# The first loads, splits and bias products in another order, and a feed-forward statistic one job later

## The chip, the cores and the metric

The kernel runs on one core of one Trainium2 chip. The metric is the device time of one execution in microseconds (us). Engines are named as in the profile: PE is TensorE, DVE is VectorE, ACT is ScalarE, POOL is GpSimd, SP is SyncE, which here only issues transfers.

## The reference, cut to what matters

The kernel computes two stacks of transformer blocks over 512 tokens with 1024 features, in float32. The part that matters here is the feed-forward network (FFN) that opens and closes each of the two layers of the first block, and once more closes the second block:

```
def rmsnorm(x, g, eps=EPS):
    y = x * rsqrt(mean(x * x, axis=-1) + eps)
    return y * g

x = x + 0.5 * (silu(rmsnorm(x, g) @ w_gate) * (rmsnorm(x, g) @ w_up)) @ w_down      # layers 0 and 1, twice each
...
rel_bias: (32 buckets, 10 heads), read by bucket of the relative position, for the attention logits
```

D_FF is 2816, that is 22 tiles of 128 columns for the gate and 22 for the up projection. Between the two FFNs of a layer lie mixers (a Fourier branch, dilated window attention, a dense differential attention). The tables of position biases are made once, at the start, from rel_bias and a 0/1 table.

## The kernel before

**Products.** Every large matrix product is done on the feature-major activations: a "job" multiplies one 1024x128 block of weights (eight tiles of 128x128) with the 512 tokens into one PSUM bank. For precision, weights and activations are each split into a high part (a rounded copy, type fp32r) and a low part (what is left), and each tile takes three matmuls: high x high, low x high, high x low (lines 646 to 648). A job is thus 24 matmuls of 512 columns.

**Weights.** Two slots, s = 0 and 1, hold the weights of two jobs. For each half of a slot, SP loads `raw` from the list `jobs` (line 482), ACT copies it to `w_hi` (`split`, line 1398), POOL subtracts to get `w_lo` (`low`, line 513), and PE may then use the half. ACT may overwrite `w_hi` only when PE has finished that half of the job before in the slot (semaphores `job_half`, `job_done`). `pump(s)` on ACT is both halves of one slot. PE waits for `lo_done` ahead of each half of a job, in order of its program.

**Banks.** A job in slot s writes bank s. DVE takes the result out (`scaled`, line 2127) and multiplies it by `rs`, the reciprocal root mean square of each token; the norm is applied after the product, so jobs can begin before `rs` exists. PE waits for that (`evac`) before it writes the bank again.

**The norm's statistic.** While an FFN's input tiles are made, ACT squares each (line 1412) and DVE sums the squares in `acc` (line 2115). `statistic` on PE (line 702) sums `acc` over the partitions with a matmul by ones, directly behind job 0 of the FFN. ACT then takes the square root (`deviation`, line 1417) and DVE the reciprocal (line 2122). In the last FFN of all (`ffn("tiles")`) the statistic is made of small matmuls inside job 0.

**The FFN on each engine.** PE: job 0, statistic, job 1, then a loop of job 0 and job 1 for each further tile, in parts of 6, 8 and 8 tiles with a down projection behind each. ACT's program for the first tile of an FFN is `before()`, `deviation()`, `pump(0)`, the silu of the gate (line 1425), and then for each further tile `pump(1)`, `upper` (m_hi, line 1430), `pump(0)`, silu. Each engine works strictly in the order of its program. DVE: reciprocal, then per tile the two `scaled`, the product (line 2144) and `lower` (m_lo, line 2137).

**The start.** SP loads the small constants, the four parts of x (512 KB each), then the weights of the first two jobs in four halves. ACT issues the transfers of the 0/1 table `hot` (33 rows of 1920), of `rel_bias`, of the lambda vectors and of an identity. PE waits for those, does one small product for lambda (line 1371) and four products of 33 rows with 512 or 384 columns (line 1374), which give the bias vectors, and then begins the first layer. ACT and DVE prepare the eight x tiles in turn: square, high part, sum, low part; ACT waits for each sum before the next square, as there is one buffer for squares. `pump(0)` stands behind the second tile, `pump(1)` behind the eighth.

Of the kernel before, what the change touches and what calls it, by code (L numbers as in the profile page):

```python
# [109 lines left out]
VEC = {0: (0, 1024), 1: (1024, 384), 2: (1408, 256), 3: (1664, 256)}  # L110
VEC_COLS = 1920
HEAD_OF = [6, 7, 8, 9, 0, 1, 2, 3, 4, 5]
KIND_OF = [0, 0, 0, 0, 1, 1, 2, 2, 3, 3]
# [32 lines left out]
def constants():  # L146

    c = {}
    k, n = np.arange(P), np.arange(S)
    a = 2 * np.pi * (k[:, None] * k[None, :] % P) / P  # L150
    j = np.arange(EVEN)
    even = 2 * np.pi * (k[:, None] * 2 * j[None, :] % S) / S
    odd = 2 * np.pi * (k[:, None] * (2 * j[None, :P] + 1) % S) / S
    even_sin, odd_sin = np.sin(even), np.sin(odd)
    even_sin[:, [0, P]] = 0
    odd_sin[0] = 1 - 2 * (j[:P] % 2)
    middle = np.zeros((P, 8, EVEN))
    for g in range(8):
        middle[g, g] = 1 - 2 * (j % 2)
    c["dft"] = np.concatenate([np.cos(a) / 256, np.sin(a) / 256, np.cos(even), np.cos(odd), even_sin, odd_sin,  # L160
                               middle.reshape(P, -1)], 1)
    hot = np.zeros((33, VEC_COLS))
    for kind, (at, size) in VEC.items():
        i = np.arange(size)
        rel, ok = ((i - 511, i < 1023), (i - 191, abs(i - 191) <= 64), (4 * (i - 127), abs(i - 127) <= 64),
                   (4 * (i - 127), (i - 127) % 4 == 0))[kind]
        hot[bucket(rel), at + i] = ok
        hot[32, at + i] = np.where(ok, 0, -1e30)
    for at, size in VEC.values():
        hot[:, at:at + size] = hot[:, at:at + size][:, ::-1].copy()  # L170
    c["hot"] = hot
# [44 lines left out]
def build(nc, jobs, x_in, small_in, mem_in, pos_in, rel_in, lam_in, dft_in, hot_in, eye_in,  # L216
          window_in, chunk_in, swap_in, rows8_in, out):
    NJ = jobs.shape[0]
    with ExitStack() as ctx:
# [3 lines left out]
        def sem(name):  # L223
# [45 lines left out]
            key_squared key_sums bc_full bc_read columns_ready fill_full fill_copied mem_loaded  # L269
            input_squared input_added mem_squared mem_added query_norms"""  # L270
        (loaded, setup_in, mixer_in, tile_squared, par_ready, vec_ready, vec_stored, tab_full, silu_done, h_done,
# [7 lines left out]
         columns_ready, fill_full, fill_copied, mem_loaded, input_squared, input_added, mem_squared, mem_added,  # L279
         query_norms) = [sem(n) for n in names.split()]  # L280
        lane_names = """rows_in cross_full chunk_terms decay_done next_ready level_full turn_copied level_done
# [29 lines left out]
        rows_z = flat[0:2, VB * S:(VB + 3) * S].rearrange("p (g n) -> p g n", g=3)  # L311
        hot = flat[0:33, 0:VEC_COLS]
        relb = pt[0:33, 4, 0:10]
        lamv = pt[0:64, 5, 0:8]
# [157 lines left out]
        def _(sp):  # L472
            sp.dma_start(small[:, :], small_in).then_inc(loaded, 16)
            for i in range(4):
                sp.dma_start(x[:, 2 * i:2 * i + 2], x_in[:, 2 * i:2 * i + 2]).then_inc(x_in_part[i], 16)

            def refill(i):
# [5 lines left out]

            refill(0)
            refill(1)
# [24 lines left out]
        def _(pool):  # L510
# [85 lines left out]

            jobs_low(0, LANE_JOBS // 2)
            for s in range(4):
# [27 lines left out]
        def _(pe):  # L626
# [757 lines left out]
        def _(act):  # L1384
# [675 lines left out]
            act.dma_start(hot, hot_in).then_inc(setup_in, 16)  # L2060
            act.dma_start(pt[0:32, 4, 0:10], rel_in).then_inc(setup_in, 16)
            act.dma_start(lamv, lam_in).then_inc(setup_in, 16)
            act.dma_start(eye[:, :], eye_in).then_inc(mixer_in, 16)
            act.wait_ge(loaded, 16)
            for k in range(KT):
                if k:
                    act.wait_ge(acc_step, k)
                if k == 2:
                    pump(0)
                prepare(k, small[:, TAIL["g_first"] + k:TAIL["g_first"] + k + 1], (x_in_part[k // 2], 16))  # L2070
                if k == 0:
                    act.wait_ge(vec_ready, 1)
                    act.activation(stats[:, 0:4], ps[6][:, 0:4], ACT.Exp).then_inc(lam_done, 1)
            pump(1)
            act.wait_ge(vec_ready, 2)
            for i in range(2):
                copy = act.activation(vec_sb[:, i * 512:i * 512 + 512], ps[2 + i][0:10, :], ACT.Copy)
            copy.then_inc(vec_copied, 1)
# [10 lines left out]
        def _(dve):  # L2089
# [11 lines left out]
            dve.memset(eps[:, 1:2], 1e-5).then_inc(par_ready, 1)  # L2101
            dve.memset(relb[32:33], 1.0).then_inc(par_ready, 1)
            dve.wait_ge(dve_step, c.now("dve"))
# [19 lines left out]

            def scaled(s, dst):

                dve.wait_ge(job_done[s], c.next(f"job{s}"))
                dve.tensor_tensor(dst, ps[s][:, :], rs[:, :], ALU.mult).then_inc(evac[s], c.up(f"evac{s}"))  # L2127

# [9 lines left out]

            def ff_tile(k):
                scaled(0, gr)  # L2140
                scaled(1, ur)
# [18 lines left out]
            def ffn(gain):  # L2160
                reciprocal_rms()
                for part, n in enumerate(FF_PARTS):
                    with c.loop(dve, n, {**JOB, "silu": 1, "h": 1, "m_hi": 1, "m": 1}) as i:
                        ff_tile(i)
                    if part < 2:
# [300 lines left out]
            def second():  # L2466
# [41 lines left out]
                for part, n in enumerate(FF_PARTS):  # L2508
                    with c.loop(dve, n, {**JOB, "silu": 1, "h": 1, "m_hi": 1, "m": 1}) as i:
                        ff_tile(i)  # L2510
                    if part == 0:
# [419 lines left out]
            for k in range(KT):  # L2931
                dve.wait_ge(x_in_part[k // 2], 16)
                prepare(k, small[:, TAIL["g_first"] + k:TAIL["g_first"] + k + 1])
            dve.wait_ge(vec_ready, 2)
            for i in range(2, 4):
                n = min(512, VEC_COLS - i * 512)
                copy = dve.tensor_copy(vec_sb[:, i * 512:i * 512 + n], ps[2 + i][0:10, 0:n])
            copy.then_inc(vec_copied, 1)
# [14 lines left out]

def arrays_of(i):
# [37 lines left out]
    for n, v in tail.items():  # L2995
# [13 lines left out]
        "pos_in": i["positions_2"],  # L3009
        "rel_in": i["rel_bias"],  # L3010
        "lam_in": np.stack([i[n][l] for l in range(2) for n in ("lam_q1", "lam_q2", "lam_k1", "lam_k2")], 1),
# [16 lines left out]
```

## Time and profile before

| | |
|---|---|
| median of 3 runs | 3389.3 us (3389.01 to 3389.61) |
| span of the profiled execution | 3389.0 us, 0.3 us below that median |
| PE busy | 3340.8 us, 99% of the span |
| POOL, DVE, ACT busy | 1568.5, 1449.3, 1351.6 us |
| HBM read | 309.64 MB |

The profiled execution's own time is taken as its span; nothing around it is known beyond the 0.3 us. Busy time of PE counts overlapping matmuls once. All times of rows are from the start of the span.

### The profile page before, as it was taken

How to read it: one execution, taken by the hardware profiler on the slowest of the kernel's cores; microseconds unless marked ns; L12 is line 12 of the kernel's file. 1: busy time of each engine (PE TensorE's matmuls, PEld its weight loads, DVE VectorE, ACT ScalarE, POOL GpSimd, SP SyncE). 2: the span in 40 equal slices, each digit the busy share in tenths (PEclk: the TensorE clock that was granted, in tenths of full speed). 3: DMA queues.
4: the chain of work that ended last, by engine and by line, in shares of the span. 5: the costliest groups of instructions: out<-in, count | busy, mean ns of one | idle time of the engine just before them, and what ended most of it. 6: DMA issues, size and time to landing. Idle time of an engine off the chain costs nothing.

```text
span 3389.0 us, 52959 instructions
## 1 busy us (share of the span) xinstructions
PE 3340.8 (99%) x16934; PEld 2729.1 (81%) x16934; DVE 1449.3 (43%) x2241; ACT 1351.6 (40%) x2414; POOL 1568.5 (46%) x1198
## 2 busy tenths in 40 slices
PE   8999999999999999999999999999999999999999
PEld 6888888788888888888888788888877787778887
DVE  4223622655322342324434644232478676342323
ACT  4323324654432343334235634332447554333332
POOL 4544443345454445444433354544433356255444
PEclk9999999999999999999999999999999999999999
DMA  3332322233232233223222233323322123123322
GB/s 124 108 97 96 118 88 69 73 103 99 96 109 96 96 97 109 96 96 119 96 75 76 68 115 97 110 94 100 98 76 71 46 73 107 50 73 109 97 96 87
DMA packets 175224, 313.65 MB, mean 93 GB/s; under 512 B 19121, under 2 KB 28337, under 8 KB 175096
## 3 DMA queue, kind: packets, MB, share of 16 engines
q1 hardware_dynamic: 163172, 298.09, 27.3%
q10 hardware_dynamic: 11924, 13.86, 1.6%
q8 instruction: 80, 1.31, 0.2%
q14 instruction: 48, 0.39, 0.0%
HBM read 309.64 MB, written 2.23 MB: 92 GB/s over the span
## 4 chain that ended last, share of the span: by engine, by line
PE 94%; DVE 2%; issue 2%; ACT 1%; POOL 1%; ACTq 0%; DMA 0%; SPq 0%; DVEq 0%; POOLq 0%
PE ps L646 25%; PE ps L648 25%; PE ps L647 25%; PE ps L685 2%; PE ps L687 2%; PE ps L686 2%; PE ps L856 1%; PE ps L667 1%; PE ps L669 1%; PE ps L668 1%; PE ps L871 1%; PE ps L1049 1%; PE ps L736 0%; PE ps L863 0%; PE ps L653 0%
## 5 line engine op out<-in xcount | busy, mean ns | idle before, releaser
L513 POOL TENSOR_TENSOR w_lo<-raw,w_hi 128x512 fp32r<-128x512 f32 x1120 | 1488.0, 1334 | 1734.3 <-ACT w_hi L1398 1729.2
L1398 ACT ACTIVATE w_hi<-raw 128x512 fp32r<-128x512 f32 x1120 | 693.4, 628 | 1293.2 <-PE ps L648 1192.7
L646 PE MATMUL ps<-u_hi,w_hi 128*128 128x512 f32 (+1 forms) x2902 | 1140.7, 393 | 7.4 <-DVE u_lo L2410 4.1
L648 PE MATMUL ps<-u_lo,w_hi 128*128 128x512 f32 (+1 forms) x2902 | 1124.8, 388 | 0.0
L647 PE MATMUL ps<-u_hi,w_lo 128*128 128x512 f32 (+1 forms) x2902 | 1124.6, 388 | 0.0
L646 PEld LDWEIGHTS ps<-u_hi,w_hi 128*128 128x128 f32 x2902 | 546.4, 188 | 129.4 <-issue 15.7
L647 PEld LDWEIGHTS ps<-u_hi,w_lo 128*128 128x128 f32 x2902 | 546.4, 188 | 113.4 <-issue 5.4
L648 PEld LDWEIGHTS ps<-u_lo,w_hi 128*128 128x128 f32 x2902 | 546.1, 188 | 112.5
L2127 DVE TENSOR_TENSOR T<-ps,rs 128x512 f32<-128x512 f32 x268 | 185.1, 691 | 733.2 <-PE ps L648 730.5
L646 PE MATMUL ps<-m_hi,w_hi 128*128 128x512 f32 x964 | 378.3, 392 | 2.4 <-DVE m_lo L2487 1.3
L647 PE MATMUL ps<-m_hi,w_lo 128*128 128x512 f32 x964 | 375.2, 389 | 0.0
L648 PE MATMUL ps<-m_lo,w_hi 128*128 128x512 f32 x964 | 375.1, 389 | 0.0
L646 PEld LDWEIGHTS ps<-m_hi,w_hi 128*128 128x128 f32 x964 | 181.0, 188 | 46.8 <-DVE m_lo L2487 5.3
L2149 DVE SCALAR_TENSOR_TENSOR x<-ps,x 128x512 f32 x112 | 77.4, 691 | 322.0 <-PE ps L648 265.2
L648 PEld LDWEIGHTS ps<-m_lo,w_hi 128*128 128x128 f32 x964 | 181.0, 188 | 37.9
L647 PEld LDWEIGHTS ps<-m_hi,w_lo 128*128 128x128 f32 x964 | 181.0, 188 | 37.5 <-issue 0.7
L2144 DVE TENSOR_TENSOR T<-T 128x512 f32<-128x512 f32 x110 | 188.0, 1709 | 20.7 <-DVE T L2127 17.4
L1430 ACT ACTIVATE m_hi<-T 128x512 f32 (+1 forms) x130 | 82.3, 633 | 277.3 <-DVE T L2144 217.3
L2137 DVE TENSOR_TENSOR m_lo<-T,m_hi 128x512 f32 (+1 forms) x130 | 92.7, 713 | 113.9 <-ACT m_hi L1430 113.9
L2127 DVE TENSOR_TENSOR pt<-ps,rs 128x512 f32<-128x512 f32 (+1 forms) x83 | 57.1, 688 | 183.0 <-PE ps L648 182.4
L687 PE MATMUL ps<-m_lo,w_hi 128*128 128x512 f32 x252 | 98.0, 389 | 0.0
L685 PE MATMUL ps<-m_hi,w_hi 128*128 128x512 f32 x252 | 98.0, 389 | 0.0
(492 smaller groups left out, 3033.8 us busy)
## 6 DMA issues: line engine op xcount, KB each, us to landing
raw<-jobs SPq DMA_DIRECT2D x1120, 256.0 KB, 2.7
tab<-vec_dram ACTq DMA_DIRECT2D x8, 448.0 KB, 5.7
pt<-rows_dram ACTq DMA_DIRECT2D x9, 256.0 KB, 4.8
x<-x_in SPq DMA_DIRECT2D x4, 512.0 KB, 6.9
out<-x SPq DMA_DIRECT2D x8, 256.0 KB, 2.3
tab<-dft_in ACTq DMA_DIRECT2D x2, 901.0 KB, 4.7
pt<-share_dram ACTq DMA_DIRECT2D x4, 384.0 KB, 4.7
T<-rows_dram ACTq DMA_DIRECT2D x3, 256.0 KB, 5.3
```

The lines of the kernel that those rows point to most:

```text
L513: pool.tensor_tensor(w_lo[:, s, w], raw[:, s, w], w_hi[:, s, w].bitcast(F32), ALU.subtract).then_inc(lo_done[s], 1)
L646: pe.matmul(ps[bank][:, 0:n], w_hi[:, s, w], hi[:, k, 0:n], start=k == ks[0], stop=False)
L647: pe.matmul(ps[bank][:, 0:n], w_lo[:, s, w], hi[:, k, 0:n], start=False, stop=False)
L648: last = pe.matmul(ps[bank][:, 0:n], w_hi[:, s, w], lo[:, k, 0:n], start=False, stop=k == ks[-1])
L685: pe.matmul(ps[s][:, :], w_hi[:, s, w], hi[:, k], start=k == 0, stop=False)
L687: last = pe.matmul(ps[s][:, :], w_hi[:, s, w], lo[:, k], start=False, stop=k == n - 1)
L1398: act.activation(w_hi[:, s, half_of(half)], raw[:, s, half_of(half)], ACT.Copy).then_inc(hi_done[s], 1)
L1430: act.activation(tile(m_hi, k), hf if src is None else src, ACT.Copy).then_inc(m_hi_done, c.up("m_hi"))
L2127: dve.tensor_tensor(dst, ps[s][:, :], rs[:, :], ALU.mult).then_inc(evac[s], c.up(f"evac{s}"))
L2137: dve.tensor_tensor(tile(m_lo, k), hf if src is None else src, tile(m_hi, k).bitcast(F32), ALU.subtract).then_inc(m_ready, c.up("m"))
L2144: dve.tensor_tensor(hf, sg, ur, ALU.mult).then_inc(h_done, c.up("h"))
L2149: dve.scalar_tensor_tensor(out=tile(x, k), in0=ps[s][:, :], scalar=scale, in1=tile(x, k), op0=ALU.mult, op1=ALU.add).then_inc(evac[s], c.u ...
```

## The change

It does three things. At the start, SP interleaves the weight halves of the first job with the parts of x, and ACT makes the high parts of all tiles, and the splits of the first job, ahead of the squares; POOL squares tiles 0 to 2 and ACT tiles 3 to 7, each into a buffer of its own. The four bias products become row tiles: the 0/1 table is cut into four strips of 480 columns that lie on 32 partitions each, so each product uses its own 32 rows of PE's array (the row for unreached positions takes the place of bucket 15, which no position has). In every FFN, the third and fourth job write banks 2 and 3 without a wait for the first pair's results, and in the FFNs of the two layers the statistic is behind job 1 instead of behind job 0. The diff, cut to its core:

```diff
@@ constants: 32 rows, four strips of 480 columns
-    hot = np.zeros((33, VEC_COLS))
+    hot = np.zeros((32, VEC_COLS))
...
+    c["hot"] = np.concatenate(np.split(hot, 4, 1))
@@ SP
-            for i in range(4):
-                sp.dma_start(x[:, 2 * i:2 * i + 2], x_in[:, 2 * i:2 * i + 2]).then_inc(x_in_part[i], 16)
+            first_weights(0, 0)
+            first_inputs(0)
+            first_inputs(1)
+            first_weights(0, 1)
+            first_inputs(2)
+            first_inputs(3)
+            first_weights(1, 0)
+            first_weights(1, 1)
-            refill(0)
@@ POOL
-            jobs_low(0, LANE_JOBS // 2)
+            first_low(0, 0)
+            first_input_square(0)
+            first_input_square(1)
+            first_low(0, 1)
+            first_input_square(2)
+            first_low(1, 0)
+            first_low(1, 1)
+            jobs_low(1, LANE_JOBS // 2)
@@ PE, ffn
-                        job(0, u_hi, u_lo, ready=ready, stat=stat)
+                        job(0, u_hi, u_lo, ready=ready, stat=stat == "tiles" and stat)
                         job(1, u_hi, u_lo)
-                    with c.loop(pe, n - (part == 0), PJOB):
+                        if stat is True:
+                            statistic()
+                        pe.wait_ge(vec_copied, 2)
+                        for s in range(2):
+                            c.take(f"evac{s}")
+                            product(s, 2 + s, u_hi, u_lo, range(KT)).then_inc(job_done[s], c.up(f"job{s}"))
+                    with c.loop(pe, n - 2 * (part == 0), PJOB):
@@ PE, start
-            pe.wait_ge(par_ready, 3)
+            pe.wait_ge(par_ready, 2)
...
-                n = min(512, VEC_COLS - i * 512)
-                mm = pe.matmul(ps[2 + i][0:10, 0:n], relb, hot[:, i * 512:i * 512 + n], start=True, stop=True)
+                rows = slice(32 * i, 32 * i + 32)
+                mm = pe.matmul(ps[2 + i][0:10, 0:VEC_STRIP], relb[rows], hot[rows], start=True, stop=True, tile_position=(32 * i, 0))
@@ ACT, start
-            for k in range(KT):
-                if k:
-                    act.wait_ge(acc_step, k)
-                if k == 2:
-                    pump(0)
-                prepare(k, ...)
+            split(0, 0)
+            for k in range(2):
+                first_upper(k)
+            act.wait_ge(vec_ready, 1)
+            act.activation(stats[:, 0:4], ps[6][:, 0:4], ACT.Exp).then_inc(lam_done, 1)
+            for k in range(2, 4):
+                first_upper(k)
+            split(0, 1)
+            for k in range(4, KT):
+                first_upper(k)
             pump(1)
+            for k in range(len(POOL_SQUARES), KT):
+                act.activation(first_square[:, k], x[:, k], ACT.Square).then_inc(square_done, c.up("square"))
@@ DVE, ffn (both places)
+                    apart = 2 if part == 0 else 0
+                    for i in range(apart):
+                        ff_tile(i, 2 * i)
+                    with c.loop(dve, n - apart, ...) as i:
+                        ff_tile(i + apart)
@@ DVE, start: all eight low parts first, then the eight sums
```

`rel_bias` is given four times over (128 rows of 10), one copy for each strip. ACT's program for the FFNs (`before()`, `deviation()`, `pump(0)`, silu) is not touched.

## Rows read from the trace of the kernel before

**Rows 1.** The page: busy time by engine, and the chain that ended last.
```profile
PE 3340.8 (99%) x16934; PEld 2729.1 (81%) x16934; DVE 1449.3 (43%) x2241; ACT 1351.6 (40%) x2414; POOL 1568.5 (46%) x1198
...
PE 94%; DVE 2%; issue 2%; ACT 1%; POOL 1%; ACTq 0%; DMA 0%; SPq 0%; DVEq 0%; POOLq 0%
```

**Rows 2.** Timeline of layer 1's first FFN: start, length, engine, line, [idle before].
```profile
1240.21 1.02 PE L702 MATMUL ps<-T,ones 128*128 128x512 f32 x2
...
1241.27 0.69 ACT L1417 ACTIVATE T<-ps,eps 128x512 f32<-128x512 f32 x1 [0.71 <-PE ps L702]
1241.30 0.40 PE L647 MATMUL ps<-u_hi,w_lo 128*128 128x512 f32 x1
...
1241.85 1.14 ACT L1398 ACTIVATE w_hi<-raw 128x512 fp32r<-128x512 f32 x2
...
1242.55 2.54 POOL L513 TENSOR_TENSOR w_lo<-raw,w_hi 128x512 fp32r<-128x512 f32 x2 [2.35 <-ACT w_hi L1398]
...
1246.62 0.49 PE L646 MATMUL ps<-u_hi,w_hi 128*128 128x512 f32 x1
...
1247.70 2.99 POOL L513 TENSOR_TENSOR w_lo<-raw,w_hi 128x512 fp32r<-128x512 f32 x2 [2.61 <-ACT w_hi L1398]
```

**Rows 3.** Timeline, PE: the second FFNs of layer 0 and of layer 1.
```profile
879.77 1.02 PE L702 MATMUL ps<-T,ones 128*128 128x512 f32 x2
...
885.66 0.39 PE L647 MATMUL ps<-u_hi,w_lo 128*128 128x512 f32 x1
885.89 0.39 PE L648 MATMUL ps<-u_lo,w_hi 128*128 128x512 f32 x1
886.15 0.49 PE L646 MATMUL ps<-u_hi,w_hi 128*128 128x512 f32 x1
...
2094.60 1.02 PE L702 MATMUL ps<-T,ones 128*128 128x512 f32 x2
...
2100.98 0.49 PE L646 MATMUL ps<-u_hi,w_hi 128*128 128x512 f32 x1
```

**Rows 4.** Timeline of the start and the first FFN.
```profile
9.50 0.56 PE L1371 MATMUL ps<-pt,ones 64*128 64x4 f32 x2 [9.50 <-DVE pt L2927]
9.98 6.57 PE L1374 MATMUL ps<-pt 33*10 33x512 f32 x8
16.48 0.80 PE L646 MATMUL ps<-u_hi,w_hi 128*128 128x512 f32 x1
...
20.06 0.60 PE L648 MATMUL ps<-u_lo,w_hi 128*128 128x512 f32 x1
20.49 0.41 PE L646 MATMUL ps<-u_hi,w_hi 128*128 128x512 f32 x1
...
22.85 1.14 DVE L2937 COPY pt<-ps 10x512 f32<-10x512 f32 x2
...
23.94 1.02 PE L702 MATMUL ps<-T,ones 128*128 128x512 f32 x2
...
31.23 0.49 PE L646 MATMUL ps<-u_hi,w_hi 128*128 128x512 f32 x1 [0.79 <-DVE T L2127]
```

**Rows 5.** Timeline, PE: two groups of eight matmul passes.
```profile
634.89 1.99 PE L856 MATMUL ps<-pt 64*128 64x512 f32 x8
...
2948.99 3.70 PE L1363 MATMUL ps<-T,pt 128*128 128x512 f32 x8 [0.69 <-ACT T L2057]
```

**Rows 6.** Stretches of two pauses of PE: PE, PEld, DVE, ACT, POOL busy, PEclk, DMA, GB/s.
```profile
2952.70:2954.10 1.40, 0.00 (x0) 0.00 (x0) 0.74 (x2) 1.09 (x2) 0.00 (x0) 1.00 0.00 0
2954.20:2957.00 2.80, 2.80 (x12) 2.08 (x12) 1.63 (x3) 0.34 (x1) 0.00 (x0) 1.00 0.00 0
...
2957.00:2959.30 2.30, 0.15 (x2) 0.01 (x1) 1.29 (x2) 1.89 (x5) 1.41 (x2) 1.00 0.00 0
2959.40:2962.80 3.40, 3.40 (x9) 2.63 (x9) 1.62 (x1) 1.01 (x2) 3.40 (x3) 0.50 0.45 152
```

**Rows 7.** Stretch of the start, same columns: transfers while x is loaded.
```profile
5.00:10.00 5.00, 0.50 (x3) 0.52 (x4) 0.81 (x4) 2.52 (x3) 0.00 (x0) 1.00 1.02 378
```

More of the change, by code:

```diff
@@ L111 @@
 VEC_COLS = 1920
+VEC_STRIP = VEC_COLS // 4
+UNREACHED = 15
 HEAD_OF = [6, 7, 8, 9, 0, 1, 2, 3, 4, 5]
@@ L167, in constants @@
         hot[bucket(rel), at + i] = ok
-        hot[32, at + i] = np.where(ok, 0, -1e30)
+        hot[UNREACHED, at + i] = np.where(ok, 0, -1e30)
     for at, size in VEC.values():
         hot[:, at:at + size] = hot[:, at:at + size][:, ::-1].copy()
-    c["hot"] = hot
+    c["hot"] = np.concatenate(np.split(hot, 4, 1))
     c["eye"] = np.eye(P)
@@ L279, in build @@
          columns_ready, fill_full, fill_copied, mem_loaded, input_squared, input_added, mem_squared, mem_added,
-         query_norms) = [sem(n) for n in names.split()]
+         query_norms, first_squares) = [sem(n) for n in names.split()]
         lane_names = """rows_in cross_full chunk_terms decay_done next_ready level_full turn_copied level_done
@@ L311, in build @@
         rows_z = flat[0:2, VB * S:(VB + 3) * S].rearrange("p (g n) -> p g n", g=3)
-        hot = flat[0:33, 0:VEC_COLS]
-        relb = pt[0:33, 4, 0:10]
+        hot = pt[:, 0, 0:VEC_STRIP]
+        relb = pt[:, 4, 0:10]
+        first_square = pt[:, 8:16]
+        POOL_SQUARES = (0, 1, 2)
         lamv = pt[0:64, 5, 0:8]
@@ L473, in _, with first_weights, first_inputs @@
             sp.dma_start(small[:, :], small_in).then_inc(loaded, 16)
-            for i in range(4):
+            def first_weights(s, half):
+                w = half_of(half)
+                sp.dma_start(raw[:, s, w], jobs[s, :, w]).then_inc(raw_full[s][half], 16)
+            def first_inputs(i):
                 sp.dma_start(x[:, 2 * i:2 * i + 2], x_in[:, 2 * i:2 * i + 2]).then_inc(x_in_part[i], 16)
+            first_weights(0, 0)
[6 more added lines that the diff above has]
+            first_weights(1, 1)
             def refill(i):
@@ L595, in lane_low, with first_low, first_input_square @@
                         memory_sum(k)
-            jobs_low(0, LANE_JOBS // 2)
+            def first_low(s, half):
+                pool.wait_ge(hi_done[s], half + 1)
+                low(s, half)
+            def first_input_square(k):
+                pool.wait_ge(x_in_part[k // 2], 16)
+                pool.tensor_tensor(first_square[:, k], x[:, k], x[:, k], ALU.mult).then_inc(first_squares, 1)
+            first_low(0, 0)
[6 more added lines that the diff above has]
+            jobs_low(1, LANE_JOBS // 2)
             for s in range(4):
@@ L2064, in _, with first_upper @@
             act.wait_ge(loaded, 16)
-            for k in range(KT):
-                if k:
-                    act.wait_ge(acc_step, k)
-                if k == 2:
-                    pump(0)
[L2070 to L2073, printed above, removed]
+            def first_upper(k):
+                act.wait_ge(x_in_part[k // 2], 16)
+                gain = small[:, TAIL["g_first"] + k:TAIL["g_first"] + k + 1]
+                act.activation(u_hi[:, k], x[:, k], ACT.Copy, scale=gain).then_inc(u_hi_done, c.up("u_hi"))
+            split(0, 0)
[8 more added lines that the diff above has]
+                first_upper(k)
             pump(1)
+            for k in range(len(POOL_SQUARES), KT):
+                act.activation(first_square[:, k], x[:, k], ACT.Square).then_inc(square_done, c.up("square"))
             act.wait_ge(vec_ready, 2)
             for i in range(2):
-                copy = act.activation(vec_sb[:, i * 512:i * 512 + 512], ps[2 + i][0:10, :], ACT.Copy)
+                copy = act.activation(vec_sb[:, i * VEC_STRIP:(i + 1) * VEC_STRIP], ps[2 + i][0:10, 0:VEC_STRIP], ACT.Copy)
             copy.then_inc(vec_copied, 1)
@@ L2122, in reciprocal_rms, with scaled @@
                 step(dve.reciprocal(rs[:, 0:n], std[:, 0:n]))
-            def scaled(s, dst):
+            def scaled(s, dst, bank=None):
                 dve.wait_ge(job_done[s], c.next(f"job{s}"))
-                dve.tensor_tensor(dst, ps[s][:, :], rs[:, :], ALU.mult).then_inc(evac[s], c.up(f"evac{s}"))
+                dve.tensor_tensor(dst, ps[s if bank is None else bank][:, :], rs[:, :], ALU.mult).then_inc(evac[s], c.up(f"evac{s}"))
             def scaled_keys(s, dst):
@@ L2137, in lower, with ff_tile @@
                 dve.tensor_tensor(tile(m_lo, k), hf if src is None else src, tile(m_hi, k).bitcast(F32), ALU.subtract).then_inc(m_ready, c.up("m"))
-            def ff_tile(k):
-                scaled(0, gr)
-                scaled(1, ur)
+            def ff_tile(k, bank=0):
+                scaled(0, gr, bank)
+                scaled(1, ur, bank + 1)
                 dve.wait_ge(evac[1], c.now("evac1"))
@@ L2162, in ffn @@
                 for part, n in enumerate(FF_PARTS):
-                    with c.loop(dve, n, {**JOB, "silu": 1, "h": 1, "m_hi": 1, "m": 1}) as i:
-                        ff_tile(i)
+                    apart = 2 if part == 0 else 0
+                    for i in range(apart):
+                        ff_tile(i, 2 * i)
+                    with c.loop(dve, n - apart, {**JOB, "silu": 1, "h": 1, "m_hi": 1, "m": 1}) as i:
+                        ff_tile(i + apart)
                     if part < 2:
@@ L2508, in second @@
                 for part, n in enumerate(FF_PARTS):
-                    with c.loop(dve, n, {**JOB, "silu": 1, "h": 1, "m_hi": 1, "m": 1}) as i:
-                        ff_tile(i)
+                    apart = 2 if part == 0 else 0
+                    for i in range(apart):
+                        ff_tile(i, 2 * i)
+                    with c.loop(dve, n - apart, {**JOB, "silu": 1, "h": 1, "m_hi": 1, "m": 1}) as i:
+                        ff_tile(i + apart)
                     if part == 0:
@@ L2932, in _ @@
                 dve.wait_ge(x_in_part[k // 2], 16)
-                prepare(k, small[:, TAIL["g_first"] + k:TAIL["g_first"] + k + 1])
+                dve.wait_ge(u_hi_done, c.next("u_hi"))
+                dve.scalar_tensor_tensor(out=u_lo[:, k], in0=x[:, k], scalar=small[:, TAIL["g_first"] + k:TAIL["g_first"] + k + 1],
+                                         in1=u_hi[:, k].bitcast(F32), op0=ALU.mult, op1=ALU.subtract).then_inc(u_ready, c.up("u"))
+            for k in range(KT):
+                if k in POOL_SQUARES:
+                    dve.wait_ge(first_squares, k + 1)
+                else:
+                    dve.wait_ge(square_done, c.next("square"))
+                if k:
+                    dve.wait_ge(acc_step, c.now("acc"))
+                dve.tensor_tensor(acc, acc, first_square[:, k], ALU.add).then_inc(acc_step, c.up("acc"))
             dve.wait_ge(vec_ready, 2)
             for i in range(2, 4):
-                n = min(512, VEC_COLS - i * 512)
-                copy = dve.tensor_copy(vec_sb[:, i * 512:i * 512 + n], ps[2 + i][0:10, 0:n])
+                copy = dve.tensor_copy(vec_sb[:, i * VEC_STRIP:(i + 1) * VEC_STRIP], ps[2 + i][0:10, 0:VEC_STRIP])
             copy.then_inc(vec_copied, 1)
@@ L2952, in _, with bias_table @@
             second()
+def bias_table(rel):
+    one = np.ones((1, rel.shape[1]), np.float32)
+    return np.concatenate([rel[:UNREACHED], one, rel[UNREACHED + 1:]] * 4)
 def arrays_of(i):
@@ L3009, in arrays_of @@
         "pos_in": i["positions_2"],
-        "rel_in": i["rel_bias"],
+        "rel_in": bias_table(i["rel_bias"]),
         "lam_in": np.stack([i[n][l] for l in range(2) for n in ("lam_q1", "lam_q2", "lam_k1", "lam_k2")], 1),
```

5 lines of the change are left out of this document (2 added, 3 removed).

## The prediction

> **What bounds the kernel now.** I read the page first: PE is busy for 99% of the span, and the chain that ended last is 94% PE [rows 1]. So time can only come from places where PE pauses or runs at a lower clock, and any new pause is paid in full, because nothing later waits for anything slower than PE. Then I read PE's waits over the whole span: near the change they are the 9.5 us before the first product and 0.79 us before the third job of the first FFN [rows 4]. The starts of the other FFNs I read as timelines [rows 2, 3]. In layer 0's second FFN the matmul after job 1 starts 0.26 us behind the last one, against 0.23 in a steady row: a pause of 0.03 us. So the wait for the first pair's results, which the extra banks remove, costs almost nothing there. The reader should look at what ACT does behind the statistic instead: it waits for PE's statistic, takes the root, and only then makes w_hi for the third job [rows 2].
>
> **The change, part by part.**
>
> *The statistic behind job 1.* ACT's program is unchanged: deviation, then pump(0). pump(0) makes the weights of the third job, so in the new order that job's weights can't be split before the statistic, and the statistic now comes directly ahead of the job. The chain is read from before, counted from the start of the statistic [rows 2]: root begins 1241.27 - 1240.21 = 1.06 us later; first split 0.58 after that (1241.85); first low part 0.70 after that (1242.55); it takes 2.54 / 2 = 1.27. So lo_done comes at 1.06 + 0.58 + 0.70 + 1.27 = 3.61, and with a semaphore's latency, for which I put 0.07, PE goes on 3.68 us after the statistic began. The root starts right behind the statistic, so the table load for it, which ACT does while it waits, stays hidden.
>
> What this costs: before, from the start of the statistic to the third job, which holds the statistic and job 1, took 886.15 - 879.77 = 6.38 us [rows 3] in layer 0's second FFN and the same, 2100.98 - 2094.60, in layer 1's second, and 1246.62 - 1240.21 = 6.41 in layer 1's first [rows 2]. Job 1 alone is 24 matmuls at the spacing of 0.227 (885.66 to 885.89 rounds to 0.23) [rows 3], 5.45. After the change it is 5.45 + 3.68 = 9.13. The loss is 2.75 + 2.75 + 2.72 = 8.2 us over these three FFNs. In the first FFN before took 31.23 - 23.94 = 7.29 [rows 4], as DVE was late there, so the loss is 9.13 - 7.29 = 1.8. Together 10.0 us. Of the 9.13 us PE stands still for about 3.68 - 0.86 = 2.8 us; 0.86 is the statistic itself: the second matmul of job 1 starts at 1241.30, less one spacing for the first, less 1240.21 [rows 2].
>
> Queued behind ACT's wait are the split of slot 0, silu, and the split of slot 1. Is the fourth job late too? Its weights need silu, which needs the reciprocal. Before, the second pair of low parts began 1247.70 - 1240.21 = 7.49 us after the statistic [rows 2], at 2.99 / 2 = 1.5 each, so the first half is there at 9.0. The third job ends at 3.68 + 5.45 = 9.13. They meet; I put 0, and 0.4 each as the upper end.
>
> *Banks 2 and 3.* They remove the pauses of 0.03 to 0.06 and the 0.8 of the first FFN, already in the differences above. The wait for vec_copied falls on copies that start at 22.85 [rows 4] and will hardly be later, while the third job comes near 30. The FFN with "tiles" keeps its statistic within job 0 and gains nothing. The loop's next job waits for the evacuation of bank 2, which DVE does while the fourth job runs: the same cover as in any steady pair.
>
> *The clock.* After a pause of 2.3 us with hardly any matmul, the granted clock was 0.50 for the 3.4 us from 2959.4, that is 1.2 instead of 2.4 GHz; after the pause of 1.4 us before 2954.1 it stayed at 1.00 [rows 6]. There are four new pauses of 2.8 us, longer than the one that led to the fall. In those 3.4 us eight matmuls ran at 0.43 instead of 0.23, a cost of 1.6. Not every pause need be followed by it and part of the low stretch may fall into the pause; I take 1.1 each, 4.4 in all, between 0 and 6.4.
>
> *The start.* Before, the bias products run from 9.98 to 16.48, eight passes, 0.85 each for 512 columns [rows 4]; everything the first job needs is there earlier but for the products themselves. Now a pass has 480 columns: 0.80. One behind another they would take 6.4; all four tiles beside each other two steps, 1.6. Row groups can overlap here: eight passes on alternating halves of 64 rows took 1.99, eight on all rows 3.70 [rows 5]. But matmuls are issued in order, and both passes of a tile use the same rows, so tile i+1 can begin only beside tile i's second pass: five steps, 4.0 us. I take this value; 1.99 over 3.70 in place of one half says that order costs something. They begin when hot, rel_bias and lambda have landed. These now compete with 256 KB of weights put ahead of x (0.7 us at 378 GB/s [rows 7]) and are 128 rows each in place of 33 and 32; I put 1.2 us later, between 0 and 2. So the first job starts at 9.98 + 1.2 + 4.0 = 15.2 in place of 16.48: a lead of 1.3, between 4.9 (9.98 + 1.6) and -1.9 (9.98 + 2 + 6.4). The first job still starts at 1.2 GHz: before it ran 4.0 us at 0.43 spacing, from 16.48 to 20.49 [rows 4]; I put the same.
> Here a rule can be weighed. The Trainium skill, "TensorE: Matmul & The Clock Gate", section "Part 3: Packing small matmuls", gives a measured 3.07 times for four row tiles of 32 rows. By that the products would take 6.4 / 3.07 = 2.1 us, an estimate, and the lead would be 3.2; the trace has no four-tile case, only the two halves.
>
> The moved work doesn't bind. POOL does a low part in 1.3 to 1.5 us, and a square should take the same; with low, two squares, low, square, low, low, the second half of job 0 is split well ahead of PE, which needs 12 matmuls of 0.43 for the first half, and slot 1 is ready about 3 us before job 1. DVE's eight low parts and eight sums are 16 operations of some 0.7 us, done near 21, while the statistic, now behind job 1, is due near 28. If that cover were gone, each late microsecond would be one of PE.
>
> **Sum.** 3389.0 + 10.0 (waits) + 4.4 (clock) - 1.3 (lead) = 3402.1 for the profiled execution; with its 0.3 below the median, 3402.4.
>
> **The rivals.**
> 1. *The four tiles run beside each other.* Two steps of 0.80: products end at 9.98 + 1.2 + 1.6 = 12.8, lead 3.7, time 3400.0. For it: the halves overlap at all. Against: two passes per tile in order. The skill's figure above belongs to it.
> 2. *The pauses come but the clock holds.* 3389.3 + 10.0 - 1.3 = 3398.0. For it: 1.4 us didn't lower it, and 2.8 is not much above 2.3. With the full lead of 4.9 it would be 3394.4, within 0.2%.
> 3. *The fourth job is late too*, as DVE and POOL get in each other's way (low parts 2.99 for two in place of 2.54). 4 x 0.4 to 1 us: 3404 to 3406.
> 4. *The other side: the weights of the third job don't wait for the statistic*, because ACT reaches pump(0) first. Then nothing is lost, the pause of 0.8 and those of 0.03 go, and so does 1.3 at the start: 3389.3 - 0.9 - 1.3 = 3387.1, and 3383.5 with the full lead. It decides if w_hi of the third job lies before the root in ACT's order. Against: before, w_hi was free to be made from the end of job 0 and still began 0.58 behind the root [rows 2].
>
> **How the numbers follow.** Chances: forecast 0.56, rival 1 0.14, rival 2 0.14 (of which 0.04 with so large a lead that it is within 0.2%), rival 3 0.10, rival 4 0.06 (half of it faster by over 0.2%, since its start could gain more than I see). 0.2% is 6.8 us, about what a measurement of this kernel can tell from no change. Slower: 0.56 + 0.14 + 0.10 + 0.10 = 0.90; same 0.07; faster 0.03. The range: from 3396, which leaves out rival 4 and the low end of rival 2, to 3407, the sum with the clock at its full 6.4 and the lead at 0 plus 1 for rival 3.
>
> **What would show it.** In the changed profile, the four statistics (line of `statistic`) are each followed by a PE idle near 2.8 us, released by POOL's w_lo; root, w_hi and w_lo follow in steps of 1.06, 0.58, 0.70. The granted clock reads 0.50 for some microseconds behind most of them. The first job starts near 15.2 us, the bias passes take near 4 us. The first u_hi matmul of job 2 in the FFN with "tiles" shows no idle. The prediction is wrong if w_hi for slot 0 starts before the root, or if the first job starts before 12 us.

## The result and the profile after

| | before | changed |
|---|---|---|
| median | 3389.45 us (4 runs) | 3403.55 us (3399.87 to 3405.85, 4 runs) |
| ratio, 95% interval | | 1.0040 (1.0028 to 1.0052) |
| span of the profiled execution | 3389.0 us | 3400.1 us (that execution took 3401.9) |

The kernel became slower by 0.4%, and the forecast of 3402.4 lies 1.2 us from the median. Over the later comparisons the kernel before spreads more than its first runs showed: 3385.8 to 3394.1 in 33 runs, median 3390.2. So differences of 1 or 2 us are read from timelines below and not from times.

The time of an execution was 1.8 to 2.3 us above its span in every run where both are on record (3401.9 against 3400.1 here). So spans are compared with spans: 3400.1 - 3389.0 = 11.1 us is what the two profiles can explain. The two medians lie 14.1 us apart, which leaves 3 us that no timeline here shows; the interval of the ratio, 9.5 to 17.6 us, holds both.

PE's two longest waits in the changed kernel (line, whom it waited for, us in total, times, longest):

```profile
PE ps L678 <- POOL w_lo L530: 13.6, 6, 2.6
PE ps L1409 <- DVE pt L2978: 10.1, 1, 10.1
```

The wait for POOL's w_lo, the low parts of the weights, was 3.0 us in two pieces before and is now 13.6 in six. Four of them, of 2.6 us each, stand behind the statistics. The timeline of layer 1's first FFN answers to [rows 2]:

```profile
1248.61 1.02 PE L734 MATMUL ps<-T,ones 128*128 128x512 f32 x2
1249.67 0.69 ACT L1455 ACTIVATE T<-ps,eps 128x512 f32<-128x512 f32 x1 [6.76 <-PE ps L734]
1250.26 1.14 ACT L1436 ACTIVATE w_hi<-raw 128x512 fp32r<-128x512 f32 x2
...
1250.95 2.50 POOL L530 TENSOR_TENSOR w_lo<-raw,w_hi 128x512 fp32r<-128x512 f32 x2 [7.59 <-ACT w_hi L1436]
...
1252.27 0.50 PE L678 MATMUL ps<-u_hi,w_hi 128*128 128x512 f32 x1 [2.64 <-POOL w_lo L530]
```

The steps are 1.06, 0.59, 0.69 and 1.32 us, 3.66 in all, and PE idles 2.64 of them. (In a merged row of two, such as the last of POOL, each takes about half: PE goes on when the first low part is there.) ACT has been idle for 6.76 us when the statistic comes: it had time for the split, but its program puts the root first.

The same timeline at the start answers to [rows 4]:

```profile
10.06 0.56 PE L1409 MATMUL ps<-pt,ones 64*128 64x4 f32 x2 [10.06 <-DVE pt L2978]
...
10.54 1.79 PE L1412 MATMUL ps<-pt 32*10 32x480 f32 x8
...
12.26 0.80 PE L678 MATMUL ps<-u_hi,w_hi 128*128 128x512 f32 x1
...
14.40 5.58 DVE L2985 SCALAR_TENSOR_TENSOR u_lo<-x,small,u_hi 128x512 fp32r<-128x512 f32 x4
...
17.68 0.50 PE L678 MATMUL ps<-u_hi,w_hi 128*128 128x512 f32 x1 [0.73 <-DVE u_lo L2985]
19.38 0.50 PE L678 MATMUL ps<-u_hi,w_hi 128*128 128x512 f32 x1 [0.73 <-DVE u_lo L2985]
...
19.91 6.25 DVE L2994 TENSOR_TENSOR T<-T,pt 128x512 f32<-128x512 f32 x8
...
26.30 1.04 PE L734 MATMUL ps<-T,ones 128*128 128x512 f32 x2
...
29.98 0.50 PE L678 MATMUL ps<-u_hi,w_hi 128*128 128x512 f32 x1 [2.64 <-POOL w_lo L530]
```

The four bias products take 1.8 us in place of 6.6, the first job starts at 12.26 in place of 16.48, and the first statistic stands at 26.30, where in the old start job 1 would have ended at 23.94 + 5.45 = 29.39 (an estimate; experiment 6 has it at 29.41). Job 0 is now held up by the low parts of x (`u_lo`, DVE): three of its tiles start late, at 15.98, 17.68 and 19.38, by 2.0 us together. The third job starts at 29.98, 1.25 us ahead of before.

Pauses and the granted clock (columns as in [rows 6]):

```profile
27.30:29.90 2.60, 0.04 (x1) 0.00 (x0) 1.99 (x7) 2.50 (x4) 1.24 (x2) 1.00 0.22 30
30.70:34.10 3.40, 3.40 (x10) 2.65 (x9) 3.14 (x4) 1.09 (x3) 0.47 (x1) 0.50 0.49 156
886.60:889.20 2.60, 0.06 (x1) 0.00 (x0) 1.78 (x1) 2.48 (x4) 1.22 (x1) 1.00 0.00 0
889.40:892.80 3.40, 3.40 (x15) 2.81 (x16) 3.15 (x4) 1.50 (x4) 1.09 (x1) 1.00 0.43 151
1249.60:1252.20 2.60, 0.03 (x1) 0.00 (x0) 1.81 (x1) 2.51 (x4) 1.25 (x2) 1.00 0.01 3
1252.70:1256.10 3.40, 3.40 (x10) 2.66 (x9) 3.02 (x4) 1.50 (x3) 1.02 (x2) 0.50 0.47 154
```

Three pauses of equal length: behind the first and the third the granted clock was 0.50 (1.2 GHz) in the 3.4 us shown and 10 matmuls fell into them, behind the second it stayed at 1.00 (2.4 GHz) with 15. The fourth, in layer 1's second FFN, was like the second (1.00, 16 matmuls in 2111.1 to 2114.5).

The difference of the two spans can be added up from the statistics. Their starts in the two timelines, in us; where the statistic moved behind job 1, the column "less job 1" takes one job (5.45) off again, so that like is compared with like:

| statistic of | before | changed | changed, less job 1 | stage before it grew by |
|---|---|---|---|---|
| layer 0 mixers | 385.68 | 386.15 | | 0.47 (from 0) |
| layer 0 second FFN | 879.77 | 885.64 | 880.19 | -0.05 |
| layer 1 first FFN | 1240.21 | 1248.61 | 1243.16 | 2.53 |
| layer 1 mixers | 1600.51 | 1607.79 | | 4.33 |
| layer 1 second FFN | 2094.60 | 2107.27 | 2101.82 | -0.06 |
| second block | 2454.75 | 2464.70 | | 2.73 |

The last column says how much longer the stage ahead of that statistic became. 9.95 us are gathered by there. The remaining 1.1 of the 11.1 arise behind the second block's statistic. That last stretch took 934.3 us before and 935.4 changed, but 932.2 to 937.6 over the twelve profiled executions of this study, with no order by edit: the kernels of experiments 5 and 6 lead at that statistic by 2.2 and 1.0 us and end 0.6 and 2.4 behind. The granted clock is low in several stretches of this part, in every one of the twelve, and they lie elsewhere each time. So the 1.1 can't be put down to the change, and much of the spread of the times may come from there.

### The profile page after: what moved, and what is told of

Read it like the earlier page. It is cut to its first block, busy times and chain, and to the rows that moved or that the text cites. A ratio compares the mean times of both kernels' runs of the same rounds, so it can differ in the third digit from the quotient of the medians.

```text
span 3400.1 us, 52494 instructions
## 1 busy us (share of the span) xinstructions
PE 3340.4 (98%) x16934; PEld 2730.5 (80%) x16934; DVE 1453.1 (43%) x2240; ACT 1349.2 (40%) x2411; POOL 1571.7 (46%) x1201
## 4 chain that ended last, share of the span: by engine, by line
PE 92%; issue 3%; DVE 2%; POOL 1%; ACT 1%; ACTq 0%; DMA 0%; DVEq 0%; POOLq 0%
PE ps L678 25%; PE ps L680 25%; PE ps L679 25%; PE ps L717 2%; PE ps L719 2%; PE ps L718 2%; PE ps L894 1%; PE ps L699 1%; PE ps L701 1%; PE ps L700 1%; PE ps L909 1%; POOL w_lo L530 1%; PE ps L1087 1%; PE ps L774 0%; PE ps L901 0%
## 5 line engine op out<-in xcount | busy, mean ns | idle before, releaser
L678 PE MATMUL ps<-m_hi,w_hi 128*128 128x512 f32 x964 | 378.6, 393 | 2.4 <-DVE m_lo L2535 1.3
L679 PE MATMUL ps<-m_hi,w_lo 128*128 128x512 f32 x964 | 375.4, 389 | 0.0
L718 PE MATMUL ps<-m_hi,w_lo 128*128 128x512 f32 x252 | 98.1, 389 | 0.0
```

What stands on the lines that cost most here:

```text
L678: pe.matmul(ps[bank][:, 0:n], w_hi[:, s, w], hi[:, k, 0:n], start=k == ks[0], stop=False)
L679: pe.matmul(ps[bank][:, 0:n], w_lo[:, s, w], hi[:, k, 0:n], start=False, stop=False)
L718: pe.matmul(ps[s][:, :], w_lo[:, s, w], hi[:, k], start=False, stop=False)
```

## The experiments

Each is compared with runs of the kernel before, taken beside it on the same chip. The line numbers are those of each kernel. The edits are cut to what matters.

**1. The statistic behind job 0 again** (rest of the change kept).

```diff
-    job(0, ..., ready=ready, stat=stat == "tiles" and stat)
+    job(0, ..., ready=ready, stat=stat)
     job(1, u_hi, u_lo)
-    if stat is True:
-        statistic()
```

> The changed kernel with one thing undone: the FFN's statistic is again behind job 0. Theory (the pause behind the statistic is the loss, ACT's root ahead of the third job's split): the four pauses of 2.6 us and the falls of the clock behind them go in the three later FFNs, -8.2 us and most of the clock's 3 to 6. In the first FFN a new wait comes: the eight sums end at 26.16 in the changed profile, while job 0 ends near 20.7, so PE waits some 5.5 us there and the third job starts near 26.3 + 0.86 + 5.45 = 32.6 instead of 29.98, with a fall of the clock likely. Time 3390 to 3393. Rival (the loss lies in banks 2 and 3 or in the start): it stays at 3399 to 3405.

Measured: 3392.82 us, ratio 1.0009 (1.0000 to 1.0018). The theory holds in both parts. The waits of 2.6 us are gone in the three later FFNs. The wait that it foresaw in the first FFN is there, and the clock was low behind it (the statistic took 2.07 in place of 1.04), so the third job starts at 33.66 and not near 32.6:

```profile
19.52 6.25 DVE L2992 TENSOR_TENSOR T<-T,pt 128x512 f32<-128x512 f32 x8
25.83 2.07 PE L734 MATMUL ps<-T,ones 128*128 128x512 f32 x2 [5.18 <-DVE T L2992]
```

So the new start makes the sums late, and this is what a statistic behind job 1 covers in the one FFN that needs it; the other three pay for it.

**2. The split of slot 0 ahead of the root.**

```diff
     before()
-    deviation()
-pump(0)
+    pump(0)
+    deviation()
 gate(gr, sg, 0, ACT.Silu)
...
```

> The changed kernel, but in ACT's FFN program the split of slot 0 comes ahead of the root. Theory A (the third job's weights are the only thing late): the pauses of 2.6 go, as do the falls of the clock: 3403.5 - 4 x 2.8 - 3 to 5 = 3387 to 3390. Theory B (the pause only moves to the fourth job, whose split still stands behind the silu, which needs the reciprocal): in the changed profile the second pair of low parts starts 7.2 us after the statistic (1255.82 - 1248.61) and the first half is ready at 8.6; the third job would end at 0.86 + 5.45 = 6.3, so PE pauses 2.3 us one job later, clock falls included: 3403.5 - 4 x 0.4 = 3402. I hold B likelier.

Measured: 3400.57, ratio 1.0035 (1.0021 to 1.0048). Theory B. In layer 1's first FFN the third job follows the statistic at once, and the pause stands one job later:

```profile
1252.03 1.02 PE L734 MATMUL ps<-T,ones 128*128 128x512 f32 x2
1252.49 0.80 PE L678 MATMUL ps<-u_hi,w_hi 128*128 128x512 f32 x1
...
1259.25 2.99 POOL L530 TENSOR_TENSOR w_lo<-raw,w_hi 128x512 fp32r<-128x512 f32 x2 [9.54 <-ACT w_hi L1436]
...
1260.59 0.50 PE L678 MATMUL ps<-u_hi,w_hi 128*128 128x512 f32 x1 [2.05 <-POOL w_lo L530]
```

In the first FFN PE also waited 1.72 us for the sums, ahead of a statistic at 28.56: this edit already brings the wait that experiment 5 shows.

**3. The FFN part of the change alone**, on the old start (the PE and DVE hunks for the FFN).

> The kernel before with only the FFN part of the change: statistic behind job 1, third and fourth job in banks 2 and 3; the start as it was. Theory: 10.0 us of waits as in the prediction (2.75, 2.75, 2.72 and 1.8 in the first FFN) plus the clock's 0 to 6.4: 3389.4 + 10.0 + 3 = 3402.5, between 3399 and 3406. The first FFN's third job starts near 23.94 + 5.45 + 3.68 = 33.1. Rival (the start holds part of the loss): below 3399.

Measured: 3406.00, ratio 1.0049 (1.0036 to 1.0063), at the upper end. The statistic came at 30.23 and not at 29.4; of that, 0.6 us is the wait ahead of the first product, 10.1 here and 9.5 in [rows 4]. The FFN part alone makes the whole loss. The new start gives some of it back in the timelines (the third job is at 33.89 here and at 29.98 in the changed kernel); in the times, 3406.00 and 3403.55, the intervals overlap.

**4. The pauses filled.**

```diff
     pe.wait_ge(vec_copied, 2)
+    if stat is True:
+        for _ in range(11):
+            pe.matmul(ps[6][:, :], u_hi[:, 0, 0:P], u_hi[:, 0], start=True, stop=True)
```

> The changed kernel with eleven more matmuls of 512 columns on PE between statistic and third job, into a bank that nobody reads; 11 x 0.227 = 2.5 us lies inside the pause of 2.6 to 2.8. Theory (low clock behind the pauses costs 1.6 us each time it falls, and pauses cause it): the clock stays at 1.00 behind all four, the time is 3389.4 + 8.2 (three later FFNs) - 1.3 (third job of the first FFN) = 3396.3, and up to 1 more where a filler delays the third job; the spread of the changed kernel's runs (6 us) shrinks to that of before (about 1 us). Rival (the clock adds nothing, the rest is something else): 3401 to 3404 as before.

Measured: 3397.39, ratio 1.0020 (1.0011 to 1.0030), against 1.0040 (1.0028 to 1.0052) for the change. The third job still waits for the same chain, 3.69 us behind the statistic, but the clock holds:

```profile
1247.31 1.02 PE L734 MATMUL ps<-T,ones 128*128 128x512 f32 x2
1247.76 3.10 PE L760 MATMUL ps<-u_hi 128*128 128x512 f32 x11
1251.00 0.50 PE L678 MATMUL ps<-u_hi,w_hi 128*128 128x512 f32 x1
```

```profile
1250.00:1253.40 3.40, 3.27 (x15) 2.37 (x14) 3.27 (x3) 1.48 (x3) 2.18 (x2) 1.00 0.26 82
```

This stretch begins in the pause, with fillers in it; in the 3.4 us from 1251.4, as far behind the third job's start as in the rows above, PEclk is 1.00 too, with 17 matmuls. It is 1.00 behind the other three statistics as well. At the second block's statistic this execution stands at 2462.00, 2.7 us ahead of the changed kernel's, whose clock had fallen twice: some 1.35 for each fall. What was wrong: the spread of the runs stayed near 6 us (3395.1 to 3400.8), and that of the kernel before is 4.8 us over the 21 runs beside them. So most of the spread isn't made by these pauses.

**5. Both splits ahead.** ACT's program for the first tile becomes: split of slot 0, root, split of slot 1, silu.

```diff
     before()
+    pump(0)
     deviation()
-pump(0)
-gate(gr, sg, 0, ACT.Silu)
+    pump(1)
+    gate(gr, sg, 0, ACT.Silu)
+    upper(0); skip(1); pump(0)
+    gate(gr, sg, 0, ACT.Silu)      # the loop over further tiles starts one later
```

> The changed kernel, with ACT's FFN program in another order for the first tile: split of slot 0, root, split of slot 1, then silu, so that neither the third nor the fourth job's weights wait for statistic or reciprocal. Theory: no pause at any of the four statistics. The third job of the first FFN then starts near 26.3 + 0.9 = 27.2 us in place of 31.23 in the kernel before: -4.0, and -0.1 for the small pauses of the other FFNs. Time 3390.7 - 4.1 = 3386.6, 3385 to 3388. Rival (the fifth job now waits for the evacuation of bank 2, as the reciprocal is 5.5 us behind the statistic): the fifth job is due 11.8 us after the statistic and that evacuation ends near 10.0, so no; if it did, 1 us for each FFN, 3390.

Measured: 3389.41, ratio 0.9994 (0.9985 to 1.0003). All four pauses behind the statistics are gone, as the theory says. The time is 2.8 us above the 3386.6 that was expected, though the interval, 3385.1 to 3391.2 in these terms, still holds it. The timeline shows what is missing: in the first FFN PE now waits for the sums.

```profile
20.05 8.08 DVE L3003 TENSOR_TENSOR T<-T,pt 128x512 f32<-128x512 f32 x8
...
22.20 2.99 POOL L530 TENSOR_TENSOR w_lo<-raw,w_hi 128x512 fp32r<-128x512 f32 x2 [2.62 <-ACT w_hi L1436]
...
28.05 1.20 DVE L3006 COPY pt<-ps 10x480 f32<-10x480 f32 x2
28.18 1.13 PE L734 MATMUL ps<-T,ones 128*128 128x512 f32 x2 [1.59 <-DVE T L3003]
...
29.38 0.49 PE L678 MATMUL ps<-u_hi,w_hi 128*128 128x512 f32 x1
```

The eight sums took 8.08 us in place of the change's 6.25, and what is new beside them are POOL's low parts for the third job. The means mix two kinds: six of the eight took 0.68 to 0.70 us, as all eight did in the change, and the two that ran beside POOL's low parts, at 22.43 and 24.15, took 1.62 and 1.59.

A second, smaller wait is one that the change itself put in, `pe.wait_ge(vec_copied, 2)` ahead of the third job. DVE's copies of the bias vectors stand behind the sums, from 28.05 to 29.25, and the third job starts at 29.38. In experiment 6 the second matmul of the third job starts 1.09 us after the statistic, here 1.53: 0.4 us more, and the same in experiments 8 and 10. In the change the copies ended at 27.28 and the third job came at 29.98, so nothing was lost. The wait for the evacuation of bank 2, the rival of the expectation, does not appear.

**6. Both splits ahead, old start** (experiment 3 with the edit of 5).

> The kernel before with the FFN part of the change and both splits ahead, and the old start. The third job of the first FFN would start at 23.94 + 5.45 + 0.86 = 30.25 in place of 31.23: -1.0 and -0.1: 3389.6. Against both_splits_ahead it gives what the new start is worth under a statistic behind job 1: 3.0 us by theory. If the two come out alike, the start gains nothing.

Measured: 3391.14, ratio 1.0002 (0.9993 to 1.0011). Its statistic in the second block stands at 2453.77, 1.0 ahead of before, as expected, and that of experiment 5 at 2452.51. In these two executions the new start is worth 1.3 and not 3.0 us. But the lambda vectors, which the first product waits for, landed at 9.67 us in experiment 5 and at 8.58 here. Over the twelve executions they landed between 8.6 and 9.8 with the old order of transfers and between 8.8 and 9.7 with the new one, so this 1.1 us is chance and not the start's doing; without it the start would be worth some 2.4 us, an estimate. The two times, 3389.41 and 3391.14, have intervals that overlap.

**7. Row tiles alone**, on the kernel before (constants, relb, the four products and their copies).

> The kernel before with only the four bias products as row tiles (strips of 480 columns on 32 rows each). Theory A (the prediction's: the products' 6.5 us set the first job's start and so the time): the changed profile has them in 1.8 us, so 3390.7 - 3 to 4 = 3387. Theory B (job 0 was bound by the pace of the low parts of x, whose last ended at 22.94, while job 0's last matmuls ran at 23.7): the first job starts earlier, near 13.9 when its w_lo is there, but ends as before: 3390.7 - 0.3 = 3390.4. I hold B likelier now.

Measured: 3389.48, ratio 0.9999 (0.9990 to 1.0008). Theory B, with the first job at 14.46:

```profile
10.34 1.79 PE L1376 MATMUL ps<-pt 32*10 32x480 f32 x8
...
22.89 0.75 DVE L2118 SCALAR_TENSOR_TENSOR u_lo<-x,small,u_hi 128x512 fp32r<-128x512 f32 x1
...
23.69 0.51 PE L648 MATMUL ps<-u_hi,w_hi 128*128 128x512 f32 x1 [0.47 <-DVE u_lo L2118]
...
24.27 0.40 PE L650 MATMUL ps<-u_lo,w_hi 128*128 128x512 f32 x1
24.50 1.02 PE L704 MATMUL ps<-T,ones 128*128 128x512 f32 x2
```

Here too the products take 1.8 us, but the statistic behind job 0 stands at 24.50, no earlier than the 23.94 of [rows 4]: job 0 now waits four times for the low parts of x, 1.9 us in all, and its last tile (23.69) comes right behind the last of them (22.89 + 0.75). The kernel before has no such wait, but little room either: the last low part ended at 22.94 and its last tile began at 23.26, 0.3 us later:

```profile
22.19 0.75 DVE L2117 SCALAR_TENSOR_TENSOR u_lo<-x,small,u_hi 128x512 fp32r<-128x512 f32 x1
...
23.26 0.39 PE L646 MATMUL ps<-u_hi,w_hi 128*128 128x512 f32 x1
```

**8. As 5, all first squares on ACT** (`POOL_SQUARES = ()` and the three POOL calls gone).

> As both_splits_ahead, but all eight first squares on ACT and none on POOL. Theory (POOL's squares and low parts slow DVE's low parts of x: four of them took 5.58 us from 14.40 in the changed profile, 1.4 each in place of 0.75, and PE waited for them twice, 1.5 in all): job 0 ends up to 1.5 earlier, 3385.1 against 3386.6, and the sums end before 24.9. Rival (the squares on ACT end later, near 20.3, and hold the sums back): the statistic waits and nothing is gained, 3386.6 to 3387.5.

Measured: 3388.98, ratio 0.9996 (0.9987 to 1.0005). The statistic came at 26.10 in place of 28.18, of which 1.3 us is a start that lay earlier (first job 11.58 in place of 12.88). PE's 0.55 of waiting within job 0 is gone, but the wait for the sums is not, 1.58: eight sums in 9.13 us, of which the three beside POOL's low parts took 1.57 to 1.78 each and the other five 0.69. Of the expectation both are in it, the theory's gain and the rival's wait. The times of 5 and 8 are 0.4 us apart, far within their intervals.

This run also bears on whether POOL slows DVE. Four low parts of x took 4.40 us here and 6.22 in experiment 5, and the second of them, which had POOL's square beside it there and nothing here, 0.74 in place of 1.52. ACT's work beside them changed too, so it isn't a test of POOL alone.

**9. The new order with the wide products**: the change, but its four products on the same 33 rows.

> The changed kernel, but the four bias products as before on the same 33 rows, one behind another, with 480 columns each: 6.4 us in place of 1.8. Theory (the new order of transfers, high and low parts makes job 0 ready early, and then the bias products bound it; each alone gains nothing): the first job starts near 17 in place of 12.26 us and ends without its 1.5 us of waits for low parts, so the first statistic comes near 29.5 in place of 26.30, and the time is 3403.5 + 3 = 3406 to 3407. Rival (job 0's end is set by something else and the tiles are worth nothing here either): 3403.5.

Measured: 3404.19, ratio 1.0038 (1.0024 to 1.0052), which can't be told from the change's 1.0040. The timeline does tell:

```profile
10.40 6.57 PE L1411 MATMUL ps<-pt 33*10 33x480 f32 x8
...
16.90 0.80 PE L678 MATMUL ps<-u_hi,w_hi 128*128 128x512 f32 x1
...
29.29 1.02 PE L734 MATMUL ps<-T,ones 128*128 128x512 f32 x2
```

The first statistic is at 29.29 in place of 26.30, the 3 us that were expected. In the time they were not seen; the intervals of both, some 4 us to each side, leave room for either, so their worth for the whole stays open to that extent.

This execution adds to what the clock does: behind all four of its pauses of 2.6 us the granted clock fell (0.50, 0.69, 0.67 and 0.69 over the 3.4 us that begin 0.1 to 0.9 us behind the start of the third job), and its statistic in the second block stands at 2471.23, 6.5 us behind the changed kernel's. 3.0 of that is the start, and two more falls at some 1.6 are about the rest. So two falls in four are not a property of the kernel: with the same pauses it was two in the change, two in experiment 3 and four here.

**10. Seven sums**: as 8, with the first sum `acc = square 0 + square 1`.

> As both_splits_act_squares, with seven sums of squares in place of eight (the first adds tile 0 and tile 1 instead of adding tile 0 to zeros). In both_splits_act_squares PE waited 1.58 us at the first statistic for the last of eight sums, 9.13 us in all, 1.14 each. Theory (DVE's sums are what ends last at the first statistic): the wait falls by 0.7 to 1.1, the statistic comes near 25.2 in place of 26.10, the time is 3388.0 in place of 3389.0, at the edge of what can be measured; the timeline decides. Rival (POOL's low parts of the third job slow whatever sums meet them, so that the sums' end stays): the statistic stays at 26.

Measured: 3387.21, ratio 0.9992 (0.9983 to 1.0001). PE no longer waits for the sums, and the statistic is 0.65 us earlier than expected:

```profile
24.55 1.12 PE L731 MATMUL ps<-T,ones 128*128 128x512 f32 x2
```

By the time of the mixers' statistic this execution leads before by 5.2 us (380.45 against 385.68), at the second block's by 3.8 (2450.93 against 2454.75): part is given back in the mixers, where PE waits 3.8 us for DVE in all, against 2.1 in before. It has the lowest time of this study, and its interval still touches 1: that it is faster than before is not shown.

## Why the prediction was right, and where it was not

**The pause behind the statistic** was the main term and was right: 3.68 us forecast from the statistic to the third job, 3.66 to 3.68 measured; 2.75 for each later FFN forecast, 2.53 and 2.73 measured in the two stages where the clock held. Experiments 1 and 5 take it away in two ways and the loss goes, experiment 3 has it alone. Experiment 2 shows what the prediction did not say: the place of slot 1's split behind the silu is in the way too, and this shows only once slot 0's split is out of it. The fourth job wasn't late in the change itself, as forecast.

**The clock**: 4.4 us forecast over four pauses, two falls in the profiled execution, 1.6 each (4.33 less 2.73 in the table). Experiment 4 shows the pauses as the cause: with them filled the clock holds. How often it falls differs from execution to execution, two to four times in the three profiles with these pauses, so 3.2 to 6.4 us; its mean over runs isn't known.

**The start** had the wrong step. The bias products, "five steps, 4.0 us", took 1.8: each tile's two passes do not hold up the next tile. Rival 1 was right on this. The Trainium skill ("TensorE: Matmul & The Clock Gate", "Part 3: Packing small matmuls") has a measured 3.07 times for four row tiles; by that the products would have taken 2.1 us, an estimate. The ratio here, for the same 1920 columns in all, is 6.57 / 1.79 = 3.7, so the trace agrees with the page in kind and is above it in size.

The 1.2 us that the transfers would lose was wrong as well: the lambda vectors landed at 9.30 against 9.20, and the first bias product came 0.6 later mostly because DVE's small operation ahead of it took 0.61 us in place of 0.15, with a square of POOL beside it. So the lead at the first job was 4.2, not 1.3.

What the prediction missed is what comes next. It took the lead at the first job for a lead of everything behind it. In before, job 0's last tile began only 0.3 us after the last low part of x was ready, so an earlier first job alone can gain no more than that, and row tiles alone gain nothing (experiment 7). "The moved work doesn't bind" was wrong too: beside POOL's work single low parts took 1.5 to 1.8 us in place of 0.74, job 0 lost 2.0 us by them, and the sums ended at 26.16, just ahead of the statistic at 26.30 and not near 21. Of the lead of 4.2, 3.1 was left at the statistic (29.39 to 26.30). "I put the same" for the slow clock of the first job missed as well (1.4 us and not 4.0), but this hardly counts: in experiment 4, with the same start, matmuls were slow for 3.1 us and the statistic came at 26.26.

**The sum** by its terms, forecast and measured in the profile: waits 10.0 and 9.8 (2.53 + 2.73 + 2.73 + 1.84, the last by 3.68 + 5.45 - 7.29); clock 4.4 and 3.2; start -1.3 and -3.1; second block 0 and 1.1. That makes 13.1 and 11.0 over 3389.0. The nearness of 3402.4 to the median 3403.55 is thus partly luck. The start gave 1.8 more than forecast, and the profiled execution was in the faster half of the four. The last step, 0.3 us from the profiled execution to the median, compared a span with a time, and these lie 1.8 us apart; by spans the forecast is 3402.1 against 3400.1. Rivals 2 to 4 are out: the clock fell, no fourth job was late, w_hi never came ahead of the root.

## What to carry to other kernels

When a statistic or any other wait is moved on one engine, read the program of every engine that waits for it: here PE's order was improved for one FFN of four while ACT's order, which puts work that is ready behind the wait, was left, and three FFNs paid 2.7 us each, and more where the clock fell. When several items queue behind such a wait, moving one ahead shifts the pause to the next; move all of them or none. Before a step at the start is made faster, look how close behind it the next supplier runs: here the low parts of x left 0.3 us of room, and the 4.8 us taken off the bias products gave nothing alone.

## What was not expected of the hardware

Four products on 32 rows each, two passes per product, began and ended within 1.79 us, against 6.57 for eight passes of as many columns on common rows (experiment 9).

DVE's operations of 0.69 to 0.75 us on 128x512 took 1.5 to 1.8 while POOL worked on tiles of that size, and POOL's own then took up to 1.75 in place of 1.3 (low parts of x at 12.70 to 17.55 in the change; sums at 22.43 and 24.15 in experiment 5). That POOL is the cause was argued from what ran beside them; experiment 8, where one such neighbour is gone and 1.52 became 0.74, speaks for it, but nothing else was held still there.

And the first matmuls of the first job are slow for a time that no edit aims at: their spacing falls from 0.43 to 0.23 us 1.4 us after the first job began in the change (at 13.68), 4.0 in before, and between 1.4 and 5.6 over the twelve executions. The column of the granted clock reads 1.00 in these stretches, so here only the spacing shows it.
